# The last joint, the router and the experts of a two-block transformer put into one program, with the router's work cut by token tiles

## The reference, cut to what matters

```python
x = x + merged @ w_out                       # "out2", the last joint
h = rmsnorm_2(x, g_ffn)                      # x * rsqrt(mean(x^2) + eps) * g
logits_g, logits_e = h @ w_grp, h @ w_exp    # 4 groups, 32 experts
# top-1 group, then top-2 of its 8 experts; gate = softmax(top 2) * p_group
x = x + sum over the 2 experts of gate * (silu(h @ w1[e]) * (h @ w3[e])) @ w2[e]
h = rmsnorm_2(x, g_ple)
x = x + sigmoid(h @ w_pg) * (p @ w_ple)      # "embedding products": p @ w_ple
out = rmsnorm_2(x, g_final)
```

## Time and profile before

| | us |
|---|---|
| median of 3 runs | 1816.34 (1815.81 to 1816.49) |
| span of the profiled execution, first to last instruction | 1813.6 |
| PE busy in the span | 1691.4 (93%) |
| DVE / ACT / POOL busy | 804.5 / 543.4 / 50.2 |
| bytes moved, mean rate | 351.74 MB, 194 GB/s |
| share of the span on the chain that ended last: PE / DMA | 16% / 13% |

### The profile page before, as it was taken

How to read it: one execution, slowest core, us unless ns; L and a number is a source line. 1 busy time by engine, 2 the same in 40 slices (tenths; PEclk the granted TensorE clock), 3 DMA queues, 4 the chain that set the end, 5 groups by cost and what they waited for, 6 DMA issues and landing times. The chain is left out here.

```text
span 1813.6 us, 20133 instructions
## 1 busy us (share of the span) xinstructions
PE 1691.4 (93%) x8179; PEld 1175.6 (65%) x8179; DVE 804.5 (44%) x1240; ACT 543.4 (30%) x899; POOL 50.2 (3%) x89
## 2 busy tenths in 40 slices
PE   2999999889999999999999999998999988988988
PEld 2788766668878888888788876766344343433446
DVE  4764467654642232365622464245243232322345
ACT  4312356742362222232532450423100000000036
POOL 0000010100000000000000000000200000000000
PEclk9989999989999999999999999999999999999999
DMA  9775310002613333221422021247899999999961
GB/s 349 234 255 166 140 70 1 2 23 94 232 47 94 107 107 110 81 94 47 162 93 93 1 93 47 96 179 305 309 426 423 427 426 426 426 426 426 426 248 47
DMA packets 87798, 351.74 MB, mean 194 GB/s; under 512 B 9926, under 2 KB 39282, under 8 KB 71577
## 3 DMA queue, kind: packets, MB, share of 16 engines
q1 hardware_dynamic: 85146, 346.08, 49.4%
q0 software_dynamic: 2560, 4.37, 0.7%
HBM read 346.03 MB, written 8.43 MB: 195 GB/s over the span
## 5 line engine op out<-in xcount | busy, mean ns | idle before, releaser
L572 DVE TENSOR_TENSOR arena<-ring,arena 128x1024 fp32r<-128x1024 f32 x120 | 146.9, 1225 | 229.5 <-ACT arena L621 206.4
L2876 PE MATMUL ex_h<-ring,u_big_tail 128*64 128x512 f32 x512 | 153.8, 610 | 15.0 <-DMA ring<-in_w 8.0
L577 PE MATMUL up_ps<-h_high,arena 128*128 128x512 f32 x352 | 138.0, 392 | 2.6 <-DVE arena L572 2.5
L578 PE MATMUL up_ps<-arena 128*128 128x512 f32 x352 | 137.6, 391 | 0.0
L579 PE MATMUL up_ps<-h_high,arena 128*128 128x512 f32 x352 | 137.5, 391 | 0.0
L621 ACT CAST arena<-ring 128x1024 fp32r<-128x1024 f32 x81 | 84.9, 1048 | 149.3 <-PE up_ps L579 82.1
L2876 PE MATMUL ex_h<-s_ab,u_big_tail 128*64 128x512 f32 x272 | 116.1, 603 | 1.5 <-DVE u_big_tail L2847 1.5
L2876 PEld LDWEIGHTS ex_h<-ring,u_big_tail 128*64 128x64 f32 x512 | 47.1, 140 | 80.3 <-issue 79.3
L3154 ACT ACTIVATE u_big_tail<-ex_h 128x512 f32<-128x512 f32 x16 | 9.6, 597 | 298.0 <-PE ex_h L2876 297.9
L2847 DVE TENSOR_TENSOR u_big_tail<-ex_x,vcol 128x512 f32<-128x512 f32 x32 | 20.6, 686 | 175.9 <-PE ex_x L2840 175.9
L2876 PE MATMUL ex_h<-w1flat,u_big_tail 128*64 128x512 f32 x160 | 73.5, 608 | 6.5 <-DMA s_ab<-in_w 6.5
(11 more groups left out here) (596 smaller groups left out, 3629.3 us busy)
## 6 DMA issues: line engine op xcount, KB each, us to landing
ring<-in_w SPq DMA_DIRECT2D x42, 2048.0 KB, 32.8
s_ab<-in_w SPq DMA_DIRECT2D x32, 2048.0 KB, 31.4
ring<-in_w_in SPq DMA_DIRECT2D x19, 2048.0 KB, 8.1
ring<-in_w_ada SPq DMA_DIRECT2D x24, 1024.0 KB, 6.9
reg_a<-in_w SPq DMA_DIRECT2D x10, 2048.0 KB, 31.8
w1flat<-in_w SPq DMA_DIRECT2D x10, 2048.0 KB
ring<-in_w_ffn_gate SPq DMA_DIRECT2D x11, 1024.0 KB, 5.4
ring<-in_w_ffn_up SPq DMA_DIRECT2D x11, 1024.0 KB, 8.6
```

Source lines behind the costliest of these rows:

```text
L572: return engine.tensor_tensor(lo, v, hi.bitcast(F32), ALU.subtract)
L577: nc.tensor.matmul(ps, x[0], y[0], start=start, stop=False)
L578: nc.tensor.matmul(ps, x[0], y[1], start=False, stop=False)
L2876: mm = nc.tensor.matmul(ps[half, :], xT[:, k, half], ws[j][:, k, cols], start=(k == 0), stop=(k == k_end - 1))
```

## The change

out2, the router and the experts become one program (`stage_rows_route` takes the place of kind "rows" and of `stage_router`); the barrier goes, and POOL clears the old semaphores on the side.

- PE turns the rows of `x` itself, without the norm factor, as soon as they are added; DVE and ACT copy a turned tile out with one instruction each. The gain is multiplied into the router's weights (one DVE instruction), the norm factor into the logits (in the copy that writes `lg`).
- The logits are made by token tiles, each as soon as its tile is turned and copied, between the products, and go back to token rows tile by tile.
- The normed rows for the gather are written on the side, tiles 0 and 1 by ACT, 2 and 3 by DVE.
- `p` and its weights are loaded before m5 instead of after the rows, and lie elsewhere, so that m8's buffer holds only the router's small tiles: m8 now waits for `listed`. m7 goes ahead of m6.
- The embedding products 0 to 2 stay ahead of the ranks, 3 behind them, 4 to 6 follow the slot lists, and product 7 follows the first turn of gathered rows.

```diff
+            for t in range(NT):                       # tensor engine
+                for h in range(2):
+                    for k in range(begin, K):
...
+                        mm = st.products(ps[h * NT + t][:], k, t, h)
+                    mm.then_inc(ready, 1)
+                if t >= 1:
+                    turn(t - 1)
+                if t == 2:
+                    router(0)
+            router(1)
+            turn(3)
+            router(2)
+            turn_p(0)
+            router(3)
+            turn_p(1)
+            pe.wait_ge(joined, 1)
+            pe.wait_ge(lg_a, NT - 1)
+            for t in range(NT - 1):
+                turn_back(t)
+            pe.wait_ge(lg_d, 1)
+            turn_back(NT - 1)
             for i in range(3):
+                early(i)
...
+            early(3)
             pe.wait_ge(placed, 3)
...
             mm.then_inc(lists, 1)
+            for i in range(4, 7):
+                early(i)
+            def router(t):
...
+                for k in range(KD):
+                    half = slice(64 * (k % 2), 64 * (k % 2) + 64)
+                    mm = nc.tensor.matmul(ps_l[t][half, 0:P], b.wr[:, k, :], hT[:, k, t * P:t * P + P], ...)
+            def split(t):                             # vector; scalar has the other half
+                dve.wait_ge(turned, 2 * t + 1)
+                nc.vector.tensor_copy(hT[:, 0:4, t * P:t * P + P], ps[t][:].rearrange(...)).then_inc(ev_d, 1)
+            square(0)                                 # scalar engine
+            square(1)
+            split(0)
+            normed(0)
+            square(2)
+            split(1)
+            normed(1)
+            logit(0)
+            split(2)
+            square(3)
+            split(3)
+            logit(1)
+            logit(2)
+            sp.wait_ge(logits, NT)                    # SP's queue
+            load_expert(b, sp, 7)
+            sp.wait_ge(b.rows_saved, 16 * NT)
             load_expert(b, sp, 6)
             for i in range(4):
+                save_product(b, sp, i)
+            sp.wait_ge(zero, 16)
+            sp.wait_ge(b.listed, 2)
+            load_expert(b, sp, 8)
+            for i in range(4, 2 * NT - 1):
                 save_product(b, sp, i)
-            for i in range(4, 2 * NT):                # tensor engine, experts
...
-                early_product(nc, b, pe, ps_early[i - 4], i).then_inc(b.ple_done, 1)
+            pe.wait_ge(b.retired, 2)
+            nc.tensor.sem_inc(b.passed, 1)
+            pe.wait_ge(b.listed, 2)
             turn(0)
+            pe.wait_ge(b.ple_out, 3)
+            early_product(nc, b, pe, ps_y[0], 2 * NT - 1).then_inc(b.ple_done, 1)
```

More of the change, by code:

```diff
@@ L1646, in stage_rows_out @@
     nc, a = b.nc, b.a
-    kind = {"out1": "mod", "down": "twice", "out2": "rows"}[name]
+    if name == "out2":
+        stage_rows_route(b, chunks)
+        return
+    kind = {"out1": "mod", "down": "twice"}[name]
     if kind == "mod":
@@ L1661, in stage_rows_out @@
     ahead = 1
-    y0 = 8 if kind == "rows" else 0
-    y = [b.s_ab[:, (y0 + 2 * t) * U:(y0 + 2 * t + 2) * U] for t in range(NT)]
+    y = [b.s_ab[:, 2 * t * U:(2 * t + 2) * U] for t in range(NT)]
     z = [b.s_ab[:, (8 + 2 * t) * U:(10 + 2 * t) * U] for t in range(NT)]
@@ L1668, in stage_rows_out @@
     eps2, r1 = b.small[:, 22:23], b.small[:, 24:28]
[L1669 to L1675, removed]
+    (h_hi, h_lo), w_ahead = arena_parts(b)
+    c0 = b.c_ffn[0] if kind == "mod" else b.c_in2[0]
+    firsts = [b.chunk(c0, j)[:, :, 0:P] for j in range(2)] if kind == "mod" else [b.chunk(c0)[:, 0:2, :]]
+    w0 = [[v.rearrange("p (k n) -> p k n", k=first.shape[1]) for v in w] for w, first in zip(w_ahead, firsts)]
     if kind == "mod":
@@ L1715, in wait_source @@
                     act.wait_ge(b.merge_used, 8)
-            elif kind == "twice":
+            else:
                 act.wait_ge(b.up_ev, k + 1)
@@ L1788, in _ @@
             for t in range(NT):
-                if t == NT - 1 and kind != "rows":
+                if t == NT - 1:
                     turn_features(0, 0, 4)
@@ L1796, in _ @@
                     mm.then_inc(ready, 1)
[L1797 to L1806, removed]
+            turn_features(0, 4, 6)
+            turn_features(1, 0, 6)
+            for t in range(2):
+                turn_features(t, 6, 8)
             for t in range(2, NT):
-                turn(t)
+                turn_features(t, 0, 8)
         @block.vector
@@ L1818, in _ @@
                 st.dve_w(dve, k)
[L1819 to L1824, removed]
+            b.wait_chunk(dve, c0)
+            for j, first in enumerate(firsts):
+                dve.wait_ge(unit_hi, j + 1)
+                last = lower(nc.vector, w0[j][1], first, w0[j][0])
+            last.then_inc(unit_lo, 1)
             def add_in(t):
@@ L1841, in invert @@
                     dve.wait_ge(inv, t + 1)
[L1842 to L1851, removed]
+                    nc.vector.tensor_scalar(y[t], z[t], inv_[:, t:t + 1], None, ALU.mult).then_inc(made, 1)
             if kind == "mod":
@@ L1893, in _ @@
                 st.act_w(act, k)
[L1894 to L1898, removed]
+            b.wait_chunk(act, c0)
+            act.wait_ge(st.used, begin)
+            for w, first in zip(w0, firsts):
+                nc.scalar.copy(w[0], first).then_inc(unit_hi, 1)
             nc.scalar.activation(spare, eps, ACT.Sqrt)
@@ L1954, in _ @@
                 return
[L1955 to L1963, removed]
+    b.h_parts, b.units_made, b.rows_ready, b.rows_late = lo, unit_lo, ready, late
 def stage_ffn_up(b):
@@ L2554, in take @@
             return v
-    short, keep, listed = Area(b.u_big), Area(b.g1row), Area(b.g2row)
+    st = b.steps
+    K, LAST = len(st.steps), 2
+    begin, ahead = K - LAST, 1
+    finished = [s for s in b.passing if s not in (st.s_hi, st.w_hi, st.lo, st.used, st.scaled)]
+    hT = b.hT
+    b.arena_open.close()
+    b.open_tail()
     b.slot = b.sb("slot", [P, 2 * NT], U32)
@@ L2586, in stage_router @@
     oh1, oh2 = oh[:, 0:NT, :], oh[:, NT:2 * NT, :]
[L2587 to L2590 removed]
+    ready, added, eps_in, sq, root, inv, made_a, made_d, turned, ev_a, ev_d, wr_clear, wr_made = (
+        b.sem(f"out2_{n}") for n in ("ready", "added", "eps", "sq", "root", "inv", "ya", "yd", "turned", "eva", "evd", "wrclear", "wrmade"))
@@ L2591, in stage_router @@
+    b.tables = tables = b.sem("ro_tables")
+    b.listed = b.sem("ro_listed")
+    logits, joined, turned_in, lg_a, lg_d, chain, expin, expd, ranks, masks, zero, lists, placed, p_in, p_turned, p_moved = (
+        b.sem(f"ro_{n}") for n in ("logits", "joined", "tlogits", "lga", "lgd", "chain", "expin", "expd", "ranks", "masks", "zero",
                                    "lists", "placed", "pin", "pturn", "pmoved"))
     b.list_zero = zero
+    b.rows_saved, wr_in = b.lasting_sem("rows_saved"), b.lasting_sem("wr_in")
@@ new lines, in router, with turn_p @@
+            def router(t):
+                pe.wait_ge(ev_a, t + 1)
+                pe.wait_ge(ev_d, t + 1)
+                if t == 0:
+                    pe.wait_ge(wr_made, 1)
+                for k in range(KD):
+                    half = slice(64 * (k % 2), 64 * (k % 2) + 64)
+                    mm = nc.tensor.matmul(ps_l[t][half, 0:P], b.wr[:, k, :], hT[:, k, t * P:t * P + P], start=(k < 2), stop=(k >= KD - 2))
+                mm.then_inc(logits, 1)
+            def turn_p(k):
+                if k == 0:
+                    pe.wait_ge(p_in, 48)
@@ new lines, in split, with normed, logit @@
+            def split(t):
+                act.wait_ge(turned, 2 * t + 2)
+                nc.scalar.copy(hT[:, 4:8, t * P:t * P + P], ps[NT + t][:].rearrange("p (k s) -> p k s", k=4)).then_inc(ev_a, 1)
+            def normed(t):
+                act.wait_ge(inv, t + 1)
+                nc.scalar.activation(y[t], b.x[:, t, :], ACT.Copy, scale=inv_[:, t:t + 1]).then_inc(made_a, 1)
+            def logit(t):
+                act.wait_ge(logits, t + 1)
+                nc.scalar.copy(lgT[:, t * P:t * P + P], ps_l[t][:, 0:P]).then_inc(lg_a, 1)
```

325 lines of the change are left out of this document (175 added, 150 removed).

## The result

The changed kernel takes 1824.87 us (median of 4 runs, 1823.25 to 1826.3) against 1816.07 (4 runs, 1813.35 to 1816.49): a ratio of 1.0051, 95% interval 1.0038 to 1.0065. It is slower by 8.8 us where 3.1 us less were forecast. The profiled execution has a span of 1822.3 us against 1813.6.

What follows compares the result with a forecast made beforehand. The end was taken to be set by when the expert-weight stream becomes continuous, at m9's issue after pair 0's h1. 2.6 us from m9 plus 0.5 behind it gave 3.1 us less, 1813.2 us against 1816.34; range 1809.0 to 1816.8.

Steps and rivals of the forecast that it cites:

- `lg` 5.8 us earlier: Router part up to the logits: `lg` starts at about 1257.4 us instead of 1263.18, with router steps of 1.1 us.
- small steps: Rival, router steps: a slower PE clock or late ACT delays `lg` by about 1.8 us; 1815.0 us; chance 0.10.
- load-bound steps: Rival, router steps: bound by weight loads, 2.9 us each, time about 1820.4 us; chance 0.05.
- 11.3 us from `lg` to the first list: DVE's chain behind the logits: same instructions, still 11.3 us, so the first list comes at 1268.7 us.
- The gather, 7.9 us from its issue: Pair 0's gather beside m8: lands 7.9 us after issue, between 4.3 and 9.9; PE idles 2.9 us.
- The clock, 1.7 us: PE behind the wait for pair 0's gather: 1.7 us charged for a lowered clock after 2.9 us of waiting.
- some 2 us of waiting: PE ahead of pair 0's turn: the clock falls only past this wait; gather landings between give 5 to 7 us.
- first rival: Pair 0's gather not held up by m8, landing within 6 us of the list: 1808.6 us; chance 0.27.
- Turn, product, h1 in 11.4 us: PE behind pair 0's gather: turn 0.9, product 7 1.8, h1 7.0, with the clock 11.4 us.
- No wait for the second gather, 0.5 us: Experts behind pair 0's h1: the second gather no longer meets m8; 0.5 us gained, 0 to 1.5.
- What the change is worth is how much earlier h1 of pair 0 is done, and no more: Start of the expert weight stream: only h1's 2.6 us earlier end, releasing m9, counts; transfers behind it keep their number.
- an end that moves by another amount than m9: Sign of being wrong, end of kernel: the end was to move by as much as m9's issue.

Runs made afterwards that it cites:

- e9: The changed kernel run again without edits, as a control for its trace; 1828.69 us in a single run.
- e1: The changed kernel with TensorE's overflow loop (branch and body) left out; 1817.83 us, ratio 1.0001 to the kernel before.
- e4: The changed kernel with m8 issued only when the first pair's gather has landed; 1818.47 us, ratio 1.0003 to the kernel before.
- e2: The changed kernel with 88 more empty instructions in TensorE's queue ahead of the jump; 1815.18 us, ratio 0.9994 to the kernel before.
- e3: The kernel before with 60 empty instructions added to TensorE's queue, nothing of the change in it; 1822.48 us, ratio 1.0028.
- e5: The changed kernel with both the edits of e2 and e4; 1809.42 us, ratio 0.9967 to the kernel before.
- e7: The kernel before with TensorE's overflow loop left out, as a control; 1814.52 us, ratio 0.9992.
- e6: e5 with embedding product 7 put ahead of the first turn of gathered rows; 1807.91 us, ratio 0.9955 to the kernel before.
- e8: The kernel before run again without edits, as a control for its trace; 1818.16 us in a single run.

## Why the prediction was wrong

Point by point, counted from the `w_out` load:

- **`lg` 5.8 us earlier: right.** 5.78 us; a router step 1.09 us where 1.1 was estimated. Neither ACT nor the weight loads held up a step, so the rivals of small steps and of load-bound steps fall.
- **11.3 us from `lg` to the first list: right.** 11.28 us. PE was free 5.3 us behind the list, 5.4 were forecast.
- **The gather, 7.9 us from its issue: mis-sized**, 11.17 us, 11.25 us in e9 and 12.23 us in e1. This is the first step that failed. Both ends of its range, 4.3 and 9.9 us, lay below what came. I counted the bytes of the gather and m8 together at full rate, as if they were served in proportion to what each has left. The runs showed the gather at 19% of the engines. The nearest row, 22 packets per us beside a full stream, had that number in it: 58 packets in 3 us are 19 per us. I read a transfer of 5 to 6 us from it and then shortened the start ahead of it from 4 us to 2. With a gather of 6.81 us, in e4, m9 goes out at 84.17 us, 3.3 us earlier than before, so the rest of this sum stands.
- **The clock, 1.7 us: right in size.** 1.04 for the turn and 0.6 for the product. It came behind 6.46 us of waiting, not 2.9, and the "some 2 us of waiting" of the first rival is no fixed limit: in e2 the clock was kept behind 2.61 us.
- **Turn, product, h1 in 11.4 us: right,** 11.3 us.
- **No wait for the second gather, 0.5 us: it came, but not at the end.** The second turn follows h1 at once, and m11 goes out 8.1 us behind m9 instead of 10.1. Yet from m9 to the load of `w_pg` it is 426.6 us, against 426.1 before: these 2 us gained nothing.
- **"What the change is worth is how much earlier h1 of pair 0 is done, and no more": this step failed, and it costs most.** m9 was 0.8 us late; the end was 6.8 us late in the stretch, "an end that moves by another amount than m9", as my own sign of being wrong had it. I looked for everything that the change moves in time and for nothing that it moves in the program. It lengthened TensorE's stream ahead of the jump by 88 instructions, from 16,262 to 16,350. That put the landing of a jump, in code which no line of the diff touches, into a block that wasn't loaded. e3 shows that 60 empty instructions do the same to the kernel before, and e2 that 88 more undo it.

The first rival (a quick gather) is refuted by the 11.17 us. None of the rivals had the loss that came: the one on the slow side named the router's weight loads, and a router step took 1.09 us, not 2.9.

Without the jump the forecast's sign would still not have been shown: e2 is the changed kernel without the pause, and 0.9994 (0.9982 to 1.0006) is no change that can be measured. The saving of the router part, 5.8 us, went into a gather that was 6.9 us longer than the 4.3 us it took before, because the change issues m8 beside it. e5 has both put right and has the gain.

## What to carry to other kernels

When a kernel has a branch on one engine, count that engine's instructions: a change that only shifts them can move the landing of a jump out of the block that is loaded ahead, and the cost, here 6 to 10 us by the medians of e1 to e3, shows up as "issue" far from the edit. If a kernel is slower for no reason that its waits show, put empty instructions ahead of the jump and run it again before explaining anything else. And a small gather that PE waits for shouldn't be issued beside a load of megabytes with long rows: here it got its share by packets, not by need, and took 11 to 12 us instead of under 7.

## What was not expected of the hardware

- The last product, always the same 32 matmuls, took 7.09 us in e1, e2, e5 and e7 and 8.78 us in the kernel before, e6 and e8, behind pauses of 1.92 to 2.63 us. The pause alone doesn't decide: 2.61 us kept the clock in e2, and 2.56 us lost it in the kernel before. This is 1.7 us of scatter in every comparison of single profiles here. The last pair's h3 adds 1.5: it took 8.41 to 8.58 us in the kernel before, e3, e4, e8 and e9 and 7.09 in the other six. Ahead of the first turn 1.76 us kept it (turn 1.12 us) and 2.09 us did not (1.28 us). Why they differ was not tried.
- From the start to the `w_out` load, executions of the same instructions differed by up to 2.6 us for the kernel before (1203.49 and 1206.10) and by 4.4 us for the changed one (1205.35 and 1209.74), while the issue of m9, counted from that load, was the same within 0.01 us in each pair. In e1, whose one edit stands far behind it, m9 was 2.1 us later than in the changed kernel.
